# A hybrid decoder layer on one core: the order of w_in's column pairs, and where the RWKV gates, key norms and the first convolution tap are computed

## The chip, the cores and the metric
One core of a Trainium2 chip runs one launch of the kernel. The metric is the device time of that launch in microseconds, the median over several runs. In the profile TensorE is PE (its weight loads PEld), VectorE is DVE, ScalarE is ACT and GpSimd is POOL; SP issues most of the weight loads.

## The reference
One inference step of one layer, for 256 prompt tokens and 8 sample tokens (264 columns together), width 2048. Two feed-forward blocks (width 5632) enclose the token mixers:

```python
p = rms_norm(x) @ w_in            # [attn q,k,v | RWKV r,k,v,w-lora,a-lora,g-lora | conv u,B,C], 6400 columns
xm = p_rwkv + (prev - p_rwkv) * mu                     # token shift
w_log = -softplus(-(w0 + tanh(wl) @ w2)) - 0.5;  decay = exp(-exp(w_log))
a = sigmoid(a0 + al @ a2);  g = sigmoid(gl) @ g2       # the gates, 768 columns each
kk = normalised(kr * k_k);  kmod = kr * (1 + (a - 1) * k_a)
S_t = S_{t-1} diag(w_t) + (S_{t-1} a_t) b_t^T + v_t k_t^T ;  y_t = S_t r_t   # a_t = -kk, b_t = kk * a
y = groupnorm(y) * ln_w + ln_b
y_rwkv = (y + sum(r * kmod * r_k) * v) * g             # the bonus
y_conv = B * conv3(C * u)
x += concat(attention, y_rwkv, y_conv) @ w_out
```

The 256 prompt tokens of the RWKV recurrence are computed in four chunks of 64: products of keys and readers (grams), the inverse of a triangular matrix in five levels of doubling, then states and outputs. The eight samples take one step of the recurrence each.

## The kernel before
The whole layer is one stream of instructions per engine, written out by hand; semaphores order the engines. Weights come from DRAM in chunks of 512 columns of K by 256 (512 KB) into a ring of four (`raw`). ScalarE rounds each chunk to its high part (`head`, L298), VectorE makes the low part (`tail`, L304), and TensorE makes three products for each 128 x 128 tile (`products`, L317 to L319). Two 128-column tiles are a pair; w_in has 25 pairs of four chunks. A pair is 96 products.

Beside w_in's pairs the engines take other work from lists keyed by the pair (`beside` in `act_in`, `dve_in`, `pe_in`); what stands at pair i is queued behind that pair's chunks on its engine. `column_pair` gives the order of the pairs: attention (0 to 5), convolution (16 to 24), the low-rank columns (15), then receptances, keys, values (6 to 14). Each pair is scaled into `pj` by `project` (L595) and, if it is of RWKV, shifted by `dve_token_shift` (L962 to L971). The attention of the samples runs beside pairs 20 to 24: value loads are issued by ScalarE (L1144), products by `pe_sample_values` (L1084) in three triples, picked by `pe_collect_values` (L1094). The convolution's taps are VectorE's (`dve_conv_taps`: tap 2 at L933, taps 1 and 0 at L935), in pair 21.

Behind w_in comes `pe_shift`, then `pe_gates` / `act_gates` / `dve_gates`: squares and head sums of the keys (L1420), 18 gate products (L1444: six decays, six a, six g) that two banks take in turn, the spread of the head norms (L1435), kk, b, the modified keys, the bonus (L1449, L1585, L1528), scans of the decays (L1561), three Exp (L1498, L1499, L1503) and the transposes of values and readers (L1466). ScalarE also rounds attention and convolution outputs for w_out here (L1163, L899), and VectorE makes their low parts (L1273, L979). Then `pe_chunks` and its partners: grams (L1667), the levels (L1691, L1694, L1702 on TensorE, L1980 on VectorE), own values (L1709), reads (L1733), states, outputs and the group norm in two parts (sums L1867, squares L1876, spread L1885, the four VectorE steps L1915 to L1925). GpSimd does the samples' recurrence on 96 x 4096 states (L1377 to L1401) from the time the keys are ready; two of its sums are VectorE's (L2005, L2007 behind level 0, L2010 behind level 3). It writes the new states in four quarters; ScalarE's heads of w_out's first four chunks wait for one quarter each. w_out's first four chunks are loaded as soon as the ring has room.

The scratch tiles are placed by hand over each other; the ring's space is reused for the states while the ring waits.

## Time and profile before

| | us |
|---|---|
| median of 3 runs | 2160.91 (2160.15 to 2162.11) |
| the profiled execution | 2158.34 |
| its span, first to last instruction | 2156.6 |
| TensorE busy in the span | 2087.8 |
| VectorE busy | 1175.5 |
| ScalarE busy | 876.1 |
| GpSimd busy | 198.3 |

The page gives busy times, the chain that ended last and the costliest groups. The trace behind it can be asked for the chain in order of time, the instructions of one engine in a stretch, who waited for whom, and a table of stretches with the granted clock of TensorE. Since the profile was taken on one execution, its times add up to 2158.34, not to the median.

### The profile page before, as it was taken

How to read it: one execution, taken by the hardware profiler on the slowest of the kernel's cores; microseconds unless marked ns; L12 is line 12 of the kernel's file. 1: busy time of each engine (PE TensorE's matmuls, PEld its weight loads, DVE VectorE, ACT ScalarE, POOL GpSimd, SP SyncE). 2: the span in 40 equal slices, each digit the busy share in tenths (PEclk: the TensorE clock that was granted, in tenths of full speed). 3: DMA queues.
4: the chain of work that ended last, by engine and by line, in shares of the span. 5: the costliest groups of instructions: out<-in, count | busy, mean ns of one | idle time of the engine just before them, and what ended most of it. 6: DMA issues, size and time to landing. Idle time of an engine off the chain costs nothing.

```text
span 2156.6 us, 44699 instructions
## 1 busy us (share of the span) xinstructions
PE 2087.8 (97%) x18380; PEld 2048.8 (95%) x18380; DVE 1175.5 (55%) x1204; ACT 876.1 (41%) x984; POOL 198.3 (9%) x176
## 2 busy tenths in 40 slices
PE   6999999999999999999997979999999999999997
PEld 5999999999999999999984879999999999999997
DVE  5555555555444545669886455555555555544442
...
GB/s 161 181 180 183 179 183 178 182 182 179 178 184 175 178 182 192 167 214 218 282 207 39 9 105 185 177 184 180 180 183 178 183 179 181 182 174 181 195 175 90
DMA packets 359389, 373.36 MB, mean 173 GB/s; under 512 B 13397, under 2 KB 351865, under 8 KB 359206
## 3 DMA queue, kind: packets, MB, share of 16 engines
...
## 4 chain that ended last, share of the span: by engine, by line
PE 91%; DVE 5%; ACT 1%; DMA 1%; issue 1%; ACTq 0%; POOL 0%; POOLq 0%; SPq 0%; DVEq 0%
PE ps L317 29%; PE ps L319 29%; PE ps L318 28%; DVE wL L304 2%; DMA raw<-in_w_in_dram 1%; PE ps L1444 1%; DVE xL L351 0%; PE ps L1691 0%; PE ps L1694 0%; PE ps L1702 0%; PE ps L1084 0%; DMA vrowa<-in_rwkv_mu_dram 0%; PE ps L1733 0%; PE ps L1718 0%; PE ps L1435 0%
## 5 line engine op out<-in xcount | busy, mean ns | idle before, releaser
L304 DVE TENSOR_TENSOR wL<-raw,wH 128x1024 fp32r<-128x1024 f32 (+1 forms) x676 | 828.5, 1232 | 858.0 <-ACT wH L298 857.6
L298 ACT ACTIVATE wH<-raw 128x1024 fp32r<-128x1024 f32 (+1 forms) x676 | 699.9, 1038 | 1000.0 <-PE ps L319 937.3
L317 PE MATMUL ps<-xH,wH 128*128 128x264 f32 x3616 | 1030.5, 285 | 10.7 <-DVE wL L304 10.6
L319 PE MATMUL ps<-xH,wL 128*128 128x264 f32 x3616 | 1028.4, 284 | 0.0
L318 PE MATMUL ps<-xL,wH 128*128 128x264 f32 x3616 | 1028.4, 284 | 0.0
L317 PEld LDWEIGHTS ps<-xH,wH 128*128 128x128 f32 x3616 | 682.4, 189 | 14.5 <-issue 12.7
L319 PEld LDWEIGHTS ps<-xH,wL 128*128 128x128 f32 x3616 | 682.3, 189 | 0.0
L318 PEld LDWEIGHTS ps<-xL,wH 128*128 128x128 f32 x3616 | 681.6, 188 | 0.2
L317 PE MATMUL ps<-hH,wH 128*128 128x264 f32 x1408 | 402.4, 286 | 0.0
L319 PE MATMUL ps<-hH,wL 128*128 128x264 f32 x1408 | 401.5, 285 | 0.0
L318 PE MATMUL ps<-hL,wH 128*128 128x264 f32 x1408 | 401.3, 285 | 0.0
L317 PEld LDWEIGHTS ps<-hH,wH 128*128 128x128 f32 x1408 | 265.0, 188 | 0.2
L318 PEld LDWEIGHTS ps<-hL,wH 128*128 128x128 f32 x1408 | 265.0, 188 | 0.0
L319 PEld LDWEIGHTS ps<-hH,wL 128*128 128x128 f32 x1408 | 264.6, 188 | 0.0
L317 PE MATMUL ps<-mixH,wH 128*128 128x264 f32 x256 | 74.1, 289 | 5.7 <-DVE wL L304 5.7
L770 POOL DMA_DIRECT2D out_dram<-yst x8 | 5.9, 744 | 761.4 <-ACT yss L486 761.4
L318 PE MATMUL ps<-mixL,wH 128*128 128x264 f32 x256 | 73.8, 288 | 0.0
L319 PE MATMUL ps<-mixH,wL 128*128 128x264 f32 x256 | 73.8, 288 | 0.0
L392 ACT ACTIVATE st<-gt 128x528 f32<-128x528 f32 x44 | 28.5, 647 | 83.5 <-DVE gt L388 83.5
L756 POOL TENSOR_TENSOR acc<-acc,sq 128x528 f32<-128x528 f32 x21 | 31.0, 1478 | 292.6 <-ACT sq L340 292.3
L758 POOL COPY acc<-sq 128x528 f32<-128x528 f32 x3 | 2.4, 799 | 575.6 <-ACT sq L340 575.6
L317 PEld LDWEIGHTS ps<-mixH,wH 128*128 128x128 f32 x256 | 49.4, 193 | 6.2 <-DVE wL L304 6.2
...
## 6 DMA issues: line engine op xcount, KB each, us to landing
raw<-in_ffn_w_gate_dram SPq DMA_DIRECT2D x176, 512.0 KB, 3.5
raw<-in_ffn_w_up_dram SPq DMA_DIRECT2D x176, 512.0 KB, 3.5
raw<-in_ffn_w_down_dram SPq DMA_DIRECT2D x128, 512.0 KB, 3.6
raw<-in_w_in_dram SPq DMA_DIRECT2D x100, 512.0 KB, 5.0
...
raw<-in_w_out_dram SPq DMA_DIRECT2D x32, 512.0 KB, 3.9
...
```

The source lines that it names most:

```text
L298: nc.scalar.activation(wH[:, k % RING, 0:nk, :], raw[:, k % RING, 0:nk, :], ACT.Copy).then_inc(S("head_made"), 1)
L304: nc.vector.tensor_tensor(wL[:, k % RING, 0:nk, :], raw[:, k % RING, 0:nk, :], wH[:, k % RING, 0:nk, :].bitcast(F32), ALU.subtract).then_i ...
L317: nc.tensor.matmul(out, wH[:, k % RING, q, cols], high, start=a, stop=False)
L318: nc.tensor.matmul(out, wH[:, k % RING, q, cols], low, start=False, stop=False)
L319: last = nc.tensor.matmul(out, wL[:, k % RING, q, cols], high, start=False, stop=b)
L392: nc.scalar.activation(st[:], gt[:], ACT.Silu).then_inc(S("silu_made"), 1)
L756: nc.gpsimd.tensor_tensor(acc[:], acc[:], sq[:, slot, :, :], ALU.add).then_inc(S("squares_added"), 1)
L758: nc.gpsimd.tensor_copy(acc[:], sq[:, 0, :, :]).then_inc(S("squares_added"), 1)
L770: pool.dma_start(yp[:, :, bass.ds(i * (2 * CW) + jj * CW, CW)], yst[:, jj, :, :]).then_inc(S(f"y_out{jj}"), 16)
L1444: nc.tensor.matmul(ps[:, 6 + m % 2, 0:N], a, b, start=True, stop=True).then_inc(S("gates_made"), 1)
```

## The change
The 25 pairs come in another order: attention, convolution, low-rank as before, then keys, values, receptances. `seat` places keys and receptances in `pj` with their places exchanged. With that, more work is put beside pairs 19 to 24, some is put behind w_in, and some of what was in the gates goes into the levels and the group norm:

- ScalarE makes the convolution's tap 2 (the first one computed, with the bias) in pair 20, VectorE tap 1 in pair 20 and tap 0 in pair 21; `dve_conv_in` goes to pair 19, the state rows' transposes too.
- ScalarE bends the low-rank columns in pair 22, squares the keys in pair 23, and in pair 24 takes their root and evicts gates 0 to 9. TensorE sums the key squares and makes gates 0 and 1 behind pair 23's products, gates 2 to 7 between the chunks of pair 24, and 8 to 11 behind it. The decay and a gates alternate, on the two halves of the array's rows. VectorE makes the reciprocal and the scan mask in pair 24.
- The third triple of sample values and two of the three collections go behind w_in. The last r pair is shifted in two parts: the samples at once, the tokens behind the grams.
- The factor of the modified keys is ScalarE's (`kf`). The splits of attention and convolution for w_out and the samples' outputs go behind level 0, the sample sums L2005 and L2007 behind level 1, the bonus terms behind level 2; the bonus product and its shift go into the group norm.
- GpSimd's twelve issues of state rows go between the second and third of its steps on the states. It loads the spread table a second time after the g gates.
- SyncE waits with the loads of w_out for the third transition, since `kf` and `rd` lie in the ring.
- `act_rwkv_head` also waits for the second spread (`head_spread` 3).

The core of the diff (places of tiles, renamed semaphores and renamed operands left out):

```diff
-        for lo, hi, shift in ((0, 6, 0), (6, 15, 10), (15, 16, 0), (16, 25, -10)):
+        for lo, hi, shift in ((0, 6, 0), (6, 15, 10), (15, 16, 0), (16, 22, -7), (22, 25, -16)):
...
+        sp.wait_ge(S("transitions_out"), 3)
...
-            20: [lambda: act_load_values(act, (0, 1, 2))],
+            20: [lambda: act_load_values(act, (0, 1, 2)), lambda: act_conv_tap(act)],
             21: [lambda: act_sample_exp(act)],
-            23: [lambda: act_load_values(act, (3, 4, 5)), lambda: act_sample_values(act, 0)],
-            24: [lambda: act_load_values(act, (6, 7)), lambda: act_sample_values(act, 1)],
+            22: [lambda: act_bend(act)],
+            23: [lambda: act_load_values(act, (3, 4, 5)), lambda: act_sample_values(act, 0),
+                 lambda: act_key_squares(act)],
+            24: [lambda: act_load_values(act, (6, 7)), lambda: act_sample_values(act, 1),
+                 lambda: act_key_root(act), lambda: act_gate(act, range(10))],
...
-        return q if q < 6 or q == 15 else q + 10 if q < 15 else q - 10
+        return q if q < 6 or q == 15 else q + 10 if q < 15 else q - 7 if q < 22 else q - 16
+
+    def seat(q):
+
+        return 2 * column_pair(q) + (-6 if 16 <= q < 19 else 6 if q >= 22 else 0)
...
-            19: [lambda: dve_key_scores(dve, (6, 7))],
-            20: [lambda: dve_sample_max(dve), lambda: dve_conv_in(dve)],
-            21: [lambda: dve_sample_probs(dve), lambda: dve_conv_taps(dve)],
-            22: [lambda: dve_turned_sample_probs(dve), lambda: dve_conv_rows(dve), lambda: dve_conv_samples(dve)],
-            23: [lambda: dve_token_shift(dve, (15, 16, 17, 18))],
-            24: [lambda: dve_token_shift(dve, (19, 20, 21, 22, 23))],
+            19: [lambda: dve_key_scores(dve, (6, 7)), lambda: dve_conv_in(dve)],
+            20: [lambda: dve_sample_max(dve), lambda: dve_conv_rows(dve), lambda: dve_conv_taps(dve, (1,))],
+            21: [lambda: dve_sample_probs(dve), lambda: dve_conv_taps(dve, (0,)), lambda: dve_conv_samples(dve)],
+            22: [lambda: dve_turned_sample_probs(dve), lambda: dve_token_shift(dve, (15, 16, 17))],
+            23: [lambda: dve_token_shift(dve, (18, 19, 20, 21))],
+            24: [lambda: dve_token_shift(dve, (22, 23)), lambda: dve_scan_mask(dve), lambda: dve_key_scale(dve)],
...
-            19: [lambda: pe_turn_key_scores(pe)],
+            19: [lambda: pe_turn_key_scores(pe), lambda: pe_turn_state_rows(pe)],
             21: [lambda: pe_turn_sample_probs(pe)],
-            20: [lambda: pe_turn_state_rows(pe)],
             22: [lambda: pe_sample_values(pe, 0)],
-            23: [lambda: pe_collect_values(pe, 0), lambda: pe_sample_values(pe, 1)],
-            24: [lambda: pe_collect_values(pe, 1), lambda: pe_sample_values(pe, 2)],
+            23: [lambda: pe_collect_values(pe, 0), lambda: pe_sample_values(pe, 1), lambda: pe_key_sums(pe),
+                 lambda: pe_gate(pe, (0, 1))],
+            24: [lambda: pe_gate(pe, (8, 9, 10, 11))],
         }
         for i in range(3, MT // 2):
             pe.wait_ge(S("projected"), i - 1)
             for k in range(4):
                 products(pe, xH, xL, CK * k, CK, 2 * (i % 2), k == 0, k == 3, IN, IN_PER, i, k)
+                if i == 24 and k < 3:
+                    pe_gate(pe, (2 * k + 2, 2 * k + 3))
...
+    def act_conv_tap(act):
+        act.wait_ge(S("conv_state"), 2)
+        for j in range(RT):
+            nc.scalar.activation(pu[:, j, 0:T], pc[:, j, 0:T], ACT.Identity, bias=vec("cb", j), scale=vec("cw", 12 + j)
+                                 ).then_inc(S("conv_head"), 1)
...
-    def dve_conv_taps(dve):
-
-        for i in (2, 1, 0):
+    def dve_conv_taps(dve, taps):
+
+        for i in taps:
+            if i == 1:
+                dve.wait_ge(S("conv_head"), RT)
             back = 2 - i
             for j in range(RT):
                 out, src = pu[:, j, back:T], pc[:, j, 0:T - back]
-                if i == 2:
-                    ins = nc.vector.tensor_scalar(out, src, vec("cw", 12 + j), vec("cb", j), ALU.mult, ALU.add)
-                else:
-                    ins = nc.vector.scalar_tensor_tensor(out, src, vec("cw", 6 * i + j), out, ALU.mult, ALU.add)
+                ins = nc.vector.scalar_tensor_tensor(out, src, vec("cw", 6 * i + j), out, ALU.mult, ALU.add)
...
+    def dve_last_samples(dve):
+
+        q = MT // 2 - 1
+        j, s = 2 * column_pair(q) - 12, seat(q)
+        dve.wait_ge(S("projected"), q + 1)
+        dve.wait_ge(S("mixed"), 2 * (q - 15))
+        keep_shift(dve, q)
+        link(nc.vector.tensor_tensor(dif[:, :, T:N], shT[:, j:j + 2, :], pj[:, s:s + 2, T:N], ALU.subtract), dve)
+        dve.wait_ge(S("shift_columns"), q - 14)
+        mix(dve, q, dif, slice(T, N))
+
+    def dve_last_tokens(dve):
+
+        v, q = nc.vector, MT // 2 - 1
+        s = seat(q)
+        x = pj[:, s:s + 2]
+        dve.wait_ge(S("head_spread"), 1)
+        dve.wait_ge(S("decay_logs"), 6)
+        linked([
+            v.tensor_tensor(dif24[:, :, 1:T], x[:, :, 0:T - 1], x[:, :, 1:T], ALU.subtract),
+            v.tensor_scalar(dif24[:, :, 0:1], x[:, :, 0:1], -1.0, None, ALU.mult),
+        ], dve)
+        mix(dve, q, dif24, slice(0, T))
...
+        pool.wait_ge(S("gates_made"), 18)
+        pool.dma_start(hs[:], t["c_spread"]).then_inc(S("gains_in"), 16)
...
+        pool_state_rows(pool)
...
+    def pe_key_sums(pe):
+
+        pe.wait_ge(S("lora_in"), 80)
+        pe.wait_ge(S("key_terms"), 6)
         for j in range(RT):
-            last = nc.tensor.matmul(ps[0:H, 0, 0:N], hd[:, 10 - 2 * j:22 - 2 * j], t2[:, j, :],
+            last = nc.tensor.matmul(ps[0:H, 5, 128:392], hd[:, 10 - 2 * j:22 - 2 * j], ksq[:, j, :],
                                     start=j == 0, stop=j == RT - 1)
         last.then_inc(S("head_sums"), 1)
...
+    def pe_gate(pe, ms):
+
+        for m in ms:
+            j = m // 2 if m < 12 else m - 12
+            if m == 0:
+                pe.wait_ge(S("lora_in"), 80)
+                pe.wait_ge(S("lora_bent"), 2)
+                pe.wait_ge(S("sample_columns"), 2)
+            if m == 12:
+                pe.wait_ge(S("state_rows"), 3)
+            elif m == 13:
+                pe.wait_ge(S("values_out"), 5)
+            elif m >= 2:
                 pe.wait_ge(S("gates_out"), m - 1)
...
+    def pe_gates(pe):
+        pe.wait_ge(S("lora_in"), 80)
+        pe.wait_ge(S("head_scale"), 1)
+        pe.wait_ge(S("gates_out"), 12)
+        for j in range(RT):
+            if j == 4:
+                pe.wait_ge(S("projected"), MT // 2)
+            last = nc.tensor.matmul(ps[:, SPREAD[j], 0:N], hs0[:, j * P:j * P + P], hn[:], start=True, stop=True)
+        last.then_inc(S("head_spread"), 1)
+        pe_collect_values(pe, 1)
+        pe_sample_values(pe, 2)
+        pe_collect_values(pe, 2)
+        pe_shift(pe)
+        pe_gate(pe, range(12, 18))
+        pe.wait_ge(S("mixed"), 14)
+        pe.wait_ge(S("kk_made"), 4)
+        turn_tokens(pe, pvr, 0, 6)
...
+    def act_key_squares(act):
+        act.wait_ge(S("mixed"), 8)
+        for j in range(RT):
+            nc.scalar.activation(ksq[:, j, :], pkr[:, j, :], ACT.Square, scale=vec("kk", j)
+                                 ).then_inc(S("key_terms"), 1)
...
+    def act_gates(act):
+        ex = nc.scalar.activation
+        act_gate(act, (10, 11))
+        act_sample_values(act, 2)
+        act.wait_ge(S("tables_in"), 32)
+        for m in Zq:
+            identity(m)
+        act_keep_picked(act)
+        act_shift(act)
+        act_gate(act, range(12, 18))
         act.wait_ge(S("decay_logs"), 7)
-        act.wait_ge(S("kk_made"), 1)
-        ex = nc.scalar.activation
         ex(aT[:, :, 0:T], aT[:, :, 0:T], ACT.Exp, scale=-DECAY).then_inc(S("decays"), 1)
-        ex(t1[:, :, 0:T], lc[:, :, 0:T], ACT.Exp, scale=DECAY).then_inc(S("decays"), 1)
+        ex(gr[:, :, 0:T], lc[:, :, 0:T], ACT.Exp, scale=DECAY).then_inc(S("decays"), 1)
+        act.wait_ge(S("chunk_used"), OUT)
+        act.wait_ge(S("gates_out"), 12)
+        for j in range(RT):
+            ex(kf[:, j, :], aa[:, j, :], ACT.Identity, bias=omk[:, j:j + 1], scale=vec("ka", j)
+               ).then_inc(S("key_terms"), 1)
         ex(svec[:, 1, :].rearrange("p (b j) -> p j b", b=NB), sw[:, :, T:N], ACT.Exp, scale=-DECAY
...
+        ex(rd[:, :, 0:T], lc[:, :, 0:T], ACT.Exp, scale=-DECAY).then_inc(S("decays"), 1)
+        act.wait_ge(S("decays"), 3)
+        act.wait_ge(S("mixed"), 20)
         stage(1)
...
+    def dve_keys(dve):
+
+        link(nc.vector.tensor_tensor(pkr[:, :, 0:T], pkr[:, :, 0:T], kf[:, :, 0:T], ALU.mult), dve)
+
+    def dve_grown_keys(dve):
+
+        nc.vector.tensor_tensor(quarters(bk[:])[:, :, :, 0:4:3, :], quarters(pairs(pkr), 2), quarters(pairs(gr), 2),
+                                ALU.mult).then_inc(S("decayed"), 1)
+
+    def dve_reads(dve):
+
+        v = nc.vector
+        link(v.memset(zero[:], 0.0), dve)
+        dve.wait_ge(S("decays"), 3)
+        link(v.tensor_copy(wc[:], rd[:, :, C - 1:T:C]), dve)
+        dve.wait_ge(S("mixed"), 22)
+        v.tensor_tensor(rd[:, :, 0:T], pr[:, :, 0:T], rd[:, :, 0:T], ALU.mult).then_inc(S("decayed"), 1)
+
+    def dve_bonus(dve):
+
+        dve.wait_ge(S("decayed"), 4)
+        for j in range(RT):
+            ins = nc.vector.scalar_tensor_tensor(pkr[:, j, :], pr[:, j, :], vec("rk", j), pkr[:, j, :], ALU.mult, ALU.mult)
+        ins.then_inc(S("bonus_made"), 1)
...
+        pe_bonus(pe, 0)
         pe_group_squares(pe, 0)
         pe_group_sums(pe, 1)
         pe_group_spread(pe, 0)
+        pe_bonus(pe, 1)
...
 def act_rwkv_head(act, part):
         act.wait_ge(S("rwkv_made"), part + 1)
+        act.wait_ge(S("head_spread"), 3)
...
+        dve_keys(dve)
+        dve.wait_ge(S("grams_made"), 2)
         dve_gram(dve, 2, Aq[0], SL, 4)
+        dve_grown_keys(dve)
         dve.wait_ge(S("grams_made"), 3)
         dve_level(dve, 1)
+        dve_gram(dve, 4, Aq[1], SL, 6)
+        dve.wait_ge(S("decays"), 3)
         dve_gram(dve, 5, Aak[0], SU, 4)
-        dve_gram(dve, 4, Aq[1], SL, 6)
         dve_gram(dve, 6, Aak[1], SU, 6)
+        dve_last_tokens(dve)
+        dve_reads(dve)
...
             if lv == 0:
+                dve_split_attention(dve)
+                dve_sample_out(dve)
+                dve_split_conv(dve)
+            if lv == 1:
                 dve.wait_ge(S("sample_parts"), 1)
                 v.tensor_reduce(smal[:, 0:C], S2[:, :, 0:C // 2], AX.X, ALU.add).then_inc(S("sample_sums"), 1)
                 dve.wait_ge(S("sample_parts"), 2)
                 v.tensor_reduce(smal[:, C:C + 2], ycat[:], AX.X, ALU.add).then_inc(S("sample_sums"), 1)
+            if lv == 2:
+                dve_bonus(dve)
+                dve_split_samples(dve)
...
+        dve_bonus_values(dve, 0)
         dve_group_scale(dve, 0)
         dve_group_centre(dve, 1)
         dve_group_gate(dve, 0)
+        dve_bonus_values(dve, 1)
```

## Rows read from the trace of the kernel before

**Rows 1.** Page, part 1: busy us, share of the span, instructions.
```profile
PE 2087.8 (97%) x18380; PEld 2048.8 (95%) x18380; DVE 1175.5 (55%) x1204; ACT 876.1 (41%) x984; POOL 198.3 (9%) x176
```

**Rows 2.** Stages; length, PE, PEld, DVE, ACT, POOL busy, clock, DMA share, GB/s.
```profile
1140.00:1165.00 25.00, 19.13 (x50) 11.38 (x49) 17.39 (x29) 13.66 (x24) 5.98 (x10) 0.73 0.03 6
1165.00:1187.00 22.00, 14.63 (x317) 12.54 (x319) 13.42 (x11) 10.34 (x16) 10.62 (x4) 0.74 0.05 15
```

**Rows 3.** Chain that ended last, in order of time: start, us, what.
```profile
1115.61 0.32 PE ps L317
...
1127.41 0.79 PE ps L1094 x8
1128.21 2.72 PE ps L1084 x12
...
1182.44 1.59 PE ps L1667 x48
...
1187.49 1.47 PE ps L1691 x6
...
1217.95 2.83 PE ps L1733 x48
...
1272.13 0.59 PE ps L317
```

**Rows 4.** TensorE's waits from 1000 to 1131: us in total, times, longest.
```profile
PE ps L317 <- DVE wL L304: 3.5, 2, 2.5
```

**Rows 5.** Timeline of VectorE: start, us, what, times.
```profile
1077.36 2.01 DVE L933 TENSOR_SCALAR pj<-pj,vcol 128x256 f32<-128x256 f32 x6
...
1174.02 1.75 DVE L1591 TENSOR_TENSOR bk<-pj,t 128x1536 f32<-128x1536 f32 x1
...
1194.43 2.27 DVE L2005 TENSOR_REDUCE smal<-S 96x64 f32<-96x2048 f32 x1
...
1209.77 1.05 DVE L1980 COPY_PREDICATED zz<-cm,ps 128x768 f32<-128x768 uint32 x1
```

**Rows 6.** Timeline of ScalarE and its queue.
```profile
1115.66 3.73 ACTq L1144 DMA_DIRECT2D vb<-in_cache_swa_v_dram  x6
...
1138.06 1.28 ACT L1481 ACT_TABLE_LOAD   x1
1139.35 0.38 ACT L1481 ACTIVATE hn<-ps 12x264 f32<-12x264 f32 x1
...
1161.84 1.48 ACT L1498 ACTIVATE aT<-aT 128x1536 f32<-128x1536 f32 x1
...
1177.08 1.63 ACT L1514 ACTIVATE early<-ps 64x768 f32<-64x768 f32 x2
...
1180.22 2.53 ACT L1528 ACTIVATE bv<-bv,vcol 128x264 f32<-128x264 f32 x6
```

**Rows 7.** Timeline of TensorE; two instructions (passes) make one float32 product.
```profile
911.83 1.94 PE L1001 MATMUL ps<-rq,cb 128*128 128x264 f32 x8
...
1144.42 5.45 PE L1435 MATMUL ps<-hn,hs 12*128 12x264 f32 x12
1149.80 10.31 PE L1444 MATMUL ps<-pj,lora 64*128 64x264 f32 x24
```

**Rows 8.** Timeline of GpSimd.
```profile
1138.51 3.96 POOL L870 DMA_DIRECT2D out_dram<-zoT  x8
...
1177.83 8.90 POOL L1377 TENSOR_TENSOR S<-S,sv 96x4096 f32<-96x4096 f32 x1 [4.44 <-DVE pj L1594]
...
1205.87 4.55 POOL L1376 TENSOR_TENSOR S<-S 96x2048 f32<-96x2048 f32 x1
```

**Rows 9.** Timeline of TensorE, group norm.
```profile
1262.99 1.98 PE L1885 MATMUL ps<-hn,hs 12*128 12x136 f32 x12 [2.00 <-DVE hn L1908]
```

**Rows 10.** Windows of TensorE alone: length, busy, clock, DMA share, GB/s.
```profile
1006.00:1008.00 2.00, 2.00 (x11) 0.50 0.78 182
```

**Rows 11.** Page, part 6: DMA issues, KB each, median us to landing.
```profile
raw<-in_w_out_dram SPq DMA_DIRECT2D x32, 512.0 KB, 3.9
```

419 lines of the change are left out of this document (211 added, 208 removed).

## The prediction
> **What bounds the kernel now.** I read the page first: TensorE is busy 97% of the span [rows 1], so the only time to be had is where it works below its pace. The stage table shows such a place: behind w_in TensorE's mean clock is 0.73 and 0.74 of full, so about half of the time at 1.2 GHz, and of those 47 us 13 hold no TensorE work at all [rows 2]. The chain of work gives the landmarks [rows 3]: pair 24's products end at 1127.4, the loop over the five levels of the inverse starts at 1187.5 (60.1 us later), w_out's first product is at 1272.1 (84.6 us after that). The change is to the 60.1 us: work that only needs keys, gates or the low-rank columns is done beside w_in, where ScalarE and VectorE have room, and what only needs receptances or attention is put off into the level loop. I follow four stretches: (a) pairs 20 to 24, (b) the end of w_in to the level loop, (c) the levels, (d) the group norm up to w_out. Before and after each stretch I ask what arrives last.
>
> **(a) Pairs 20 to 24.** TensorE waits for VectorE's tails here in only two places, 3.5 us in all, and 2.5 of it once [rows 4]: in pair 21, behind 18 tap instructions and the sample probabilities. The first tap (6 instructions, 2.0 us [rows 5]) goes to ScalarE, whose Identity with a bias costs about 0.42 each (6 in 2.53 us [rows 6]). Tap 1 goes into pair 20, and there VectorE now waits for ScalarE's six, which are queued behind nine issues of value loads (at 3.73 us for six [rows 6], 5.6 us). So VectorE leaves pair 20 some 0.7 us late and the 2.5 us wait shrinks by 0.8, not by 2.0. Ends: 0 and 2.5. If it grew, the cover would have to be gone in pair 21 again; I see no room for more than 0.5 us of loss.
> Added to TensorE: six head sums of key squares and gates 0 to 7 before pair 24's last product, gates 8 to 11 behind it. A 264-column float32 product of two passes takes 1.94/4, overhang off 0.45 us, at full clock [rows 7]. Head sums: 6 x 0.45 = 2.7 us. Gates 0 to 7: 8 x 0.45 = 3.6 us.
> Added wait: gate 2 needs gate 0's bank back from ScalarE. In this pair ScalarE first issues six value loads, 1115.7 to 1119.4 [rows 6], copies sample values (0.6), loads the Sqrt table (1.28 [rows 6]) and takes the root (0.4), loads the Sigmoid table (1.28) and evicts (0.5): ready at 1119.4+0.6+1.7+1.8 = 1123.5. TensorE arrives there at 1115.6 + 2.7 + 0.9 (gates 0, 1) + 2.95 (a fourth of a pair: 1115.6 to 1127.4 [rows 3]) = 1122.1, with the same 0.8 taken off both. So a stall of 1.4, with semaphores 1.7 us; ends 0 and 4. Behind the waiting gate stand three quarters of pair 24, and nobody else. ScalarE's eviction of later gates (0.5 each, two per 2.95 us) is hidden.
> The Trainium skill ("ScalarE: Activation LUTs", section What ACT_TABLE_LOAD costs) gives 1.28 us for a load and as much as 1.38 us of drain before it. By the page the stall would be 2.8 us longer. The row has the load alone, with the next activation right behind it [rows 6], so the trace does not show the drain on an engine that has run dry.
> Sum of (a): -0.8 + 2.7 + 3.6 + 1.7 = +7.2: pair 24's products end at 1134.6 instead of 1127.4.
> The head sums, gates, key squares and the root leave stretch (b), where they ran at a worse clock: the spreads took 5.45 for six products and twelve gates 10.31 [rows 7], against 2.7 and 5.4 at full clock.
>
> **(b) From there to the level loop.** TensorE: gates 8 to 11, 1.8 + 0.3 for the eviction, then six spreads 2.7 (1139.4), picking sample values 0.8, the last two samples' values 2.7 (both at their duration in the chain [rows 3]): 1142.9. From here ScalarE is the engine that arrives last, and I add up its queue: copy 0.6, two identities 1.6, picked values 0.5, three state row copies 0.7, six g gates 4.4 (taken between 0.5 and 0.9 each; 0.86 is what they cost at half clock [rows 7]), Exp table 1.28, two Exp over all tokens 2.9 (1.48 each [rows 6]), six key factors 2.5, a small and a third Exp 1.6, two stages of values 3.2 (1.63 each [rows 6]), two reader copies and one of sample vectors 2.0. Small copies are put at the 0.25 to 0.8 that their size gives at the rate of the rows. Sum 21.3, with 0.7 of latencies: 1164.9 when the last values are staged. VectorE's scans, kk, bT and the readers fit beside that: they need 3.6 + 2.6 + 1.8 + 1.8 us after 1135.5 and are wanted at 1152. The first gram is at 1163.3; VectorE then has, on the path, level 0 (1.1), keys (1.75), the mask of a gram (0.95) and the grown keys (1.75 [rows 5]), with latencies 1169; then two grams of keys, 1.59 each [rows 3], with a mask between them: level loop at 1172.4. The last r pair's token part and the reads (4.2 us) stand behind it on VectorE and cost level 0 what I count in (c).
> The clock: TensorE has four lines of low-row products and waits here, and in the kernel before it ran at 1.2 GHz for half of this time. Up to 1142.9 I priced full clock. If it falls before the sample values, they and the spreads cost up to 5.4 more. I take 1.5 (nearest is the row of spreads at 5.45 behind similar gates). Level loop at 1173.9: 13.6 us earlier than 1187.5. Ends: 9 and 17.
> The rule for pairs of gates: an even gate uses rows 0 to 63 of the array and an odd one rows 64 to 127, in two banks. The Trainium skill ("TensorEngine Tiling (Array Packing)", section When to Use Tiling) has two such products run side by side. By the page ten gates would cost 2.2 us less. No row here has this pair of forms at this size, so the sum doesn't use it.
>
> **(c) The levels.** In the kernel before, the reads of chunk 0 began at 1218.0 [rows 3], 30.5 us after the level loop's start. VectorE now has between levels: the split of attention, sample outputs and the split of the convolution (1.2 + 0.6 + 1.9 against a pause of 3.2 us), and at the start the reads. That costs 0.4 + 0.7 + 0.35 = 1.4 us. The bonus products (2.6) fit into the pause behind level 2.
> GpSimd is what I expect to arrive last. Its state work starts with the grown keys, 3.3 us before the level loop (before: 9.7 us before it, 1177.83 [rows 8]). Two passes 8.9 + 4.55 [rows 8], then the twelve issues of state rows, moved into this chain: eight take 3.96 [rows 8], twelve 6.1. Then 0.5, and again 8.95 + 4.55. Third part ready at -3.3 + 13.5 + 6.1 + 0.5 + 13.6 + 0.4 of latencies = 30.8 us after the loop's start. VectorE waits for it behind level 3, with the last level's copies queued behind: reduce 2.27, copy 1.05 [rows 5], so TensorE can start the reads at +34.2, against +30.5 before: 3.7 us given back, the 1.4 within it. Ends 1.4 (GpSimd in time) and 6. What hides the rest is the product of own values, which needs no copy of level 4. The vectors' way through DRAM and back starts at 1162, with the first reader copies, and I take it to end before the grown keys are made.
> GpSimd's last state write ends 53 us behind that third part, at 1258 with its landing; ScalarE needs it only for w_out's fourth chunk, after 1262. It stays hidden by 4 us or more.
> SyncE: w_out's first four loads no longer start during pair 23 but with the third transition, 25 us before w_out. A load of 512 KB lands 3.9 us after its issue [rows 11]; four, at 1.5 to 2 us of issue each, are there after some 10 us. Hidden by 15 us; without cover each microsecond late would be one lost.
>
> **(d) Group norm.** The bonus product, its value product and its shift move here. Part 0 is hidden in waits of TensorE (1.6 us), VectorE (1.0) and ScalarE (1.6) for each other. Part 1 puts TensorE's 1.6 us ahead of the second squares, VectorE's 1.0 ahead of the reciprocal; the second spread, which took 1.98 and ended at 1265.0 [rows 9], ends 1.0 later, and ScalarE now waits for it before the first head (0.85), which had hung on VectorE's products alone. Sum +1.9; ends 1 and 3.5.
>
> **Sum.** 13.6 - 3.7 - 1.9 = 8.0 us earlier at w_out; nothing behind it changes. The profiled execution took 2158.34 (span 2156.6 and 1.7 around it), so 2150.3; the median of the runs is 2160.91, 2.6 higher, and a timed run should show 2152.9.
>
> **Rivals.**
> Rival 1, more gain: gate pairs overlap, no stall, clock stays full up to the sample values. 2.2 + 1.7 + 1.5 more, with GpSimd's chain moving along: 13.4 us, 2147.5. For it: nothing in w_in fell below full clock in pairs 21 to 24. Against: twelve gates in 10.31 us [rows 7] show no overlap. 0.10.
> Rival 2, little gain: TensorE or ScalarE in (b) slower than added up (every handover costs more, spreads and sample values at half clock, +5), GpSimd another 2 us late. Gain about 1 to 3 us, 2159. 0.15.
> Rival 3, slower: low-row gates and the stall at gate 2 put TensorE's clock at 1.2 GHz in pair 24. The trace has this: behind a pause ahead of pair 16, weight products ran at clock 0.50 [rows 10], 11 in 2 us instead of 19. Pair 24 has 96 products, at half speed 11.8 us more. It decides from 8 us of products at half clock, two thirds of the pair; then +4 us, 2165. Against: three quarters of the time between gates is dense products, and the sample values between pairs 22 and 23 lowered nothing. 0.07.
> That the change does nothing is a part of rival 2: (b) is shortened only as far as ScalarE's queue lets it.
>
> **How the numbers follow.** My forecast (gain 4.5 to 11, 2150 to 2156.5) has 0.68. The range reaches from rival 1's time to 2159, taking in the unknown costs of (b) and (c) and rival 2's nearer half; it leaves out about 0.19. About 0.2% (4.3 us) is what a measurement of this kernel can tell from no change. Faster: 0.68 + 0.10 = 0.78; within: 0.15; slower: 0.07.
>
> **What would show it.** Pair 24 with one wait of 1 to 2 us for a gate's eviction and its products' end 7 us later than before; level loop about 39 us behind that; VectorE's third reduce waiting for GpSimd for 4 to 6 us and TensorE for 2 ahead of the reads; the second group spread 1 us later. It would be wrong if TensorE's clock is half in pair 24, if ScalarE isn't the last to arrive at 1165, or if GpSimd starts its state work later than the grown keys.

## The result, and the profile after

The changed kernel takes 2185.35 us (median of 4 runs, 2184.43 to 2187.75) against 2160.95 for the kernel before (4 runs, 2160.15 to 2162.11): ratio 1.0114, 95% interval 1.0097 to 1.0132. It is slower by 24.4 us, where 8 us less was forecast and 2159.0 was the range's upper end. The profiled execution took 2184.43 us, with a span of 2182.7.

The page's first part, to be laid beside [rows 1]: TensorE has the same work, and the span grew around it.

```profile
PE 2086.6 (96%) x18392; PEld 2050.0 (94%) x18392; DVE 1198.5 (55%) x1197; ACT 883.9 (40%) x1009; POOL 199.2 (9%) x177
```

The stage table says in which stretch. Columns: window, its length, busy time and instructions of TensorE, its weight loads, VectorE, ScalarE and GpSimd, TensorE's granted clock, DMA share, GB/s. First the kernel before: from pair 24's last product to the level loop, from there to the reads of chunk 0, from there to w_out.

```profile
1127.40:1187.50 60.10, 44.26 (x420) 28.86 (x419) 39.43 (x62) 32.67 (x52) 20.66 (x20) 0.76 0.14 35
1187.50:1218.00 30.50, 28.61 (x1118) 25.30 (x1120) 16.03 (x14) 16.86 (x22) 25.63 (x6) 0.97 0.01 2
1218.00:1272.10 54.10, 41.64 (x712) 36.55 (x712) 25.42 (x35) 15.75 (x23) 39.91 (x27) 0.93 0.11 31
```

The same three stretches of the kernel after:

```profile
1138.50:1182.20 43.70, 29.07 (x380) 20.12 (x379) 24.13 (x34) 23.25 (x38) 7.96 (x7) 0.75 0.18 46
1182.20:1242.10 59.90, 32.48 (x1121) 28.43 (x1118) 52.74 (x33) 17.02 (x22) 45.75 (x27) 0.75 0.01 3
1242.10:1297.80 55.70, 43.79 (x738) 38.89 (x736) 27.25 (x37) 19.40 (x35) 32.88 (x19) 0.93 0.21 68
```

The way to the level loop became 16.4 us shorter, as intended, and the last stretch 1.6 us longer, as forecast. The levels went from 30.5 to 59.9 us, at nearly the same number of TensorE products. VectorE is busy there for 52.7 us instead of 16.0: that is the cell to stop at, since what moved there adds up to some 10 us at its former durations. TensorE's waits in the levels (us in total, times, longest) name the same engine:

```profile
PE ps L1808 <- DVE zz L2133: 25.7, 2, 17.6
```

Two waits, 8.1 and 17.6 us, for the masks with which VectorE closes a level. The timelines of VectorE and of GpSimd (start, us, what, times) show what it did ahead of those masks:

```profile
1183.16 5.46 DVE L1022 TENSOR_TENSOR dif<-pj 128x510 f32<-128x510 f32 x1
1188.54 4.41 DVE L1023 TENSOR_SCALAR dif<-pj 128x2 f32<-128x2 f32 x1
...
1197.67 1.32 DVE L1337 TENSOR_TENSOR mixL<-pj,mixH 128x1024 fp32r<-128x1024 f32 x1
...
1210.67 20.97 DVE L1709 SCALAR_TENSOR_TENSOR pj<-pj,vcol 128x264 f32<-128x264 f32 x6
```
```profile
1179.13 8.93 POOL L1444 TENSOR_TENSOR S<-S,sv 96x4096 f32<-96x4096 f32 x1 [4.20 <-DVE bk L1693]
1188.14 4.78 POOL L1443 TENSOR_TENSOR S<-S 96x2048 f32<-96x2048 f32 x1
1192.87 0.58 POOL L885 DMA_DIRECT2D out_dram<-zoT  x1
...
1207.68 8.91 POOL L1451 TENSOR_TENSOR S<-S,sv 96x4096 f32<-96x4096 f32 x1 [7.74 <-DVE smal L2168]
1216.67 4.52 POOL L1443 TENSOR_TENSOR S<-S 96x2048 f32<-96x2048 f32 x1
1221.15 8.98 POOL L1453 TENSOR_TENSOR S<-S,sv 96x4096 f32<-96x4096 f32 x1
```

A product with a constant over **two columns takes 4.41 us**, and it ends (1192.95) where GpSimd's halving ends (1192.92). The subtraction before it ends 0.6 us, its own normal duration, behind GpSimd's first product. Once GpSimd only issues DMAs (from 1192.87) the next instructions of VectorE take their normal time. The six bonus instructions take 21 us beside three large GpSimd instructions, where 2.6 was forecast.

### The profile page after: what moved, and what is told of

The parts are those of the page before. It is cut to its first block and busy times, and to the rows that moved or that the text cites. A ratio compares the mean times of both kernels' runs of the same rounds, so it can differ in the third digit from the quotient of the medians.

```text
span 2182.7 us, 44753 instructions
## 1 busy us (share of the span) xinstructions
PE 2086.6 (96%) x18392; PEld 2050.0 (94%) x18392; DVE 1198.5 (55%) x1197; ACT 883.9 (40%) x1009; POOL 199.2 (9%) x177
## 5 line engine op out<-in xcount | busy, mean ns | idle before, releaser
L324 PE MATMUL ps<-xH,wH 128*128 128x264 f32 x3616 | 1031.6, 285 | 12.8 <-DVE wL L311 12.8
```

What stands on the lines that cost most here:

```text
L324: nc.tensor.matmul(out, wH[:, k % RING, q, cols], high, start=a, stop=False)
```

## The experiments

**Theory 1**: a VectorE instruction that takes its tensors from SBUF can't run beside a GpSimd instruction and waits for its end. **Theory 2**: those instructions wait for data. **Theory 3**: GpSimd's own chain sets the end. Each experiment is an edit of the kernel after, where nothing else is said. The ratios below are against the kernel before on the same chip (there 2159.8 to 2162.5).

**Move the waits, one at a time.** The last pair's token shift and the reads go ahead of the first gram, where VectorE is idle for 4.8 us:

```diff
         dve.wait_ge(S("decayed"), 2)
+        dve_last_tokens(dve)
+        dve_reads(dve)
         dve.wait_ge(S("grams_made"), 1)
...
-        dve_last_tokens(dve)
-        dve_reads(dve)
         for lv in range(LEVELS):
```


> The kernel after with VectorE's token shift of the last pair (L1022, L1023, L982) and its scaling of the reads (L1703) moved from behind the last gram to ahead of the first, into VectorE's 4.8 us of waiting for the first gram. Theory 1, a shared way to memory: a VectorE instruction that takes its operands from SBUF cannot run beside a GpSimd tensor instruction and waits for its end. Then 5.46 and 4.41 us of L1022 and L1023 become 0.7 and 0.2, TensorE's 8.1 us wait in level 0 goes, but the splits behind level 0 now fall on GpSimd's halving and wait for its end, and level 1 waits for GpSimd's small product behind its ten DMA issues: about 5 us less, 2180 us; the bonus still takes 21 us. Theory 2, data: the two instructions wait for a value of the last pair that comes late; then they take as long in the new place, the first gram's masks move out by it, and the time is 2185 or more. Theory 3, the order of GpSimd's own work sets the end: GpSimd's chain starts no earlier, so the time stays at 2185.

2179.37 us (ratio 1.0089, 1.0072 to 1.0105): 6 less than after, where theories 2 and 3 had nothing or a loss. The two instructions take 0.69 and 0.16 us in the new place, and the first level's mask starts 4.2 us behind the level loop's start instead of 13.7. The wait turned up where theory 1 puts it: the split behind level 0 took 5.03 us instead of 1.32 and ended 1.1 us, about its own duration, behind GpSimd's halving.

The bonus, moved from behind level 2 to behind level 1:

```diff
             if lv == 1:
+                dve_bonus(dve)
                 dve.wait_ge(S("sample_parts"), 1)
...
             if lv == 2:
-                dve_bonus(dve)
                 dve_split_samples(dve)
```


> The kernel after with the bonus product (L1709, six instructions) moved from behind level 2 to behind level 1, ahead of the reduction for which GpSimd waits, so that GpSimd has nothing under way. Theory 1 (shared way to memory): the six take 2.6 us in place of 21, TensorE's 17.6 us wait in level 3 goes, level 2 starts 2 us later, and the next to be late is the second half-sum of the sample state, for which VectorE waits some 6 us behind level 3: 12 us less, 2173 us. Theory 2 (data): the six wait for something late and do so in the new place too, 2185 or more. Theory 3 (GpSimd's chain alone sets the end): it becomes 2.6 us longer, 2188.

2176.07 us (ratio 1.0073, 1.005 to 1.0096; the runs spread from 2170.4 to 2180.6): 9 less, 3 short of theory 1, and again not the 2185 or more of theories 2 and 3. The six take 2.51 us. The missing 3 us are the 32-column sample split that stayed behind level 2: it took 7.14 us, until GpSimd's product was over, and so made level 3 late.

Both moves, with the sample split moved too:

> The kernel after with both moves: the last pair's token shift and the reads ahead of the first gram (VectorE's idle 4.8 us), bonus and the 32-column sample split behind level 1 ahead of the reduction. Theory 1 (shared way): of TensorE's two waits of 8.1 and 17.6 us neither stays; what stays is about 4 us in level 1 (the splits behind level 0 wait for the end of GpSimd's halving) and 2 us in level 4 (VectorE waits behind level 3 for GpSimd's second half-sum). From the start of the levels to the reads 39 us instead of 60: w_out starts 17 to 20 us earlier, 2166 us. Rival: GpSimd's own chain, whose last sample state must be out before w_out's first tiles are split, sets the end: it ends 12 to 14 us after what theory 1 gives for TensorE, and the time is 2173.

2165.40 us (ratio 1.0024, 1.0015 to 1.0034): theory 1 said 2166. The two moves are worth some 20 of the 24.4 us. The two lines are VectorE's wait for GpSimd's second half-sum behind level 3, which 2 us of TensorE's wait follow, and the split that still falls on the halving.

```profile
1191.50 4.30 DVE L1337 TENSOR_TENSOR mixL<-pj,mixH 128x1024 fp32r<-128x1024 f32 x1
...
1218.75 2.28 DVE L2175 TENSOR_REDUCE smy<-S 96x64 f32<-96x2048 f32 x1 [6.11 <-POOL S L1443]
```

**The other way round: the wait put into the kernel before.** One added instruction of two columns:

```diff
                 v.tensor_reduce(smy[:], S2[:, :, 0:C // 2], AX.X, ALU.add).then_inc(S("sample_sums"), 1)
+                linked([v.tensor_tensor(shT[:, 0, 0:2], shT[:, 0, 0:2], shT[:, 0, 2:4], ALU.mult)], dve)
```


> The kernel before with one VectorE instruction added behind level 3 and its reduction: a product of two columns by two columns in SBUF, on scratch (normally 0.2 us). Theory 1 (shared way): at that point GpSimd runs its third 8.9 us product (1210.4 to 1219.3), so the added instruction starts at about 1213 and ends only at 1219.4; level 4's masks, due at 1214, come 5.4 us late: 2166 us. Theory 2 (the waits of the kernel after are data waits, and such an instruction costs its duration): 2161.

2166.39 us (ratio 1.0023, 1.0009 to 1.0036), so 4 to 5 us for it. The profiled execution was the slowest of the seven, 2173.34: it was 7.6 us behind the profile of before already at the level loop, where the two programs are the same, and 7.5 us more at w_out (2.7 in the levels, 4.8 behind them, where TensorE's clock was 0.50 after a wait of 2.5 us). Its rows are good for the durations, not for the price. VectorE's and GpSimd's timelines:

```profile
1218.50 2.26 DVE L2010 TENSOR_REDUCE smy<-S 96x64 f32<-96x2048 f32 x1
1220.69 6.41 DVE L2011 TENSOR_TENSOR shT<-shT 128x2 f32<-128x2 f32 x1
```
```profile
1218.16 8.92 POOL L1385 TENSOR_TENSOR S<-S,sv 96x4096 f32<-96x4096 f32 x1
```

The reduction beside the same GpSimd product takes its normal 2.26 us; the two columns end with that product. Theory 2 has nothing to say to this.

**Change the length of GpSimd's instructions**, VectorE's program untouched:

```diff
-        step(g.tensor_tensor(S2[:], S1[:], key(0), ALU.mult))
+            for k in range(4):
+                r = slice(k * 16, k * 16 + 16)
+                ins = g.tensor_tensor(out[:, r, :], S1[:, r, :], sv[:, q, :].unsqueeze(1).broadcast_to([96, 16, C]),
+                                      ALU.mult)
```


> The kernel after with GpSimd's three products over the whole sample state (8.9 us each) cut into four instructions each and its halvings (4.7 us) into two; VectorE's program is untouched. Theory 1 in its strict form (each VectorE instruction that needs the way waits for the GpSimd instruction under way, and gets in between two): L1022 and L1023 fall from 5.46 and 4.41 us to 2.5 or less each, the six bonus instructions from 21 us to at most six times 2.4, some 13: 10 to 13 us less, 2173 us. If VectorE instead waits until GpSimd's whole run of work is over, nothing changes. Theory 2 (data) and theory 3: no change, or 1 us more for the added instructions.

2183.70 us (ratio 1.0112, 1.0095 to 1.0129): 1.7 less, hardly to be told from nothing, where theory 1 said 12. In the profiles the levels are 3.7 us shorter (56.2), and their loop starts 2.1 later. The mechanism was right, the sum was not:

```profile
1185.33 1.06 DVE L1022 TENSOR_TENSOR dif<-pj 128x510 f32<-128x510 f32 x1
1186.31 2.33 DVE L1023 TENSOR_SCALAR dif<-pj 128x2 f32<-128x2 f32 x1
1188.67 5.00 DVE L982 SCALAR_TENSOR_TENSOR pj<-dif,vcol,pj 128x256 f32<-128x256 f32 x2
1193.63 0.11 DVE L1712 MEMSET zero<- 128x64 f32 x1
1193.78 2.11 DVE L1714 COPY wc<-rd 128x24 f32<-128x24 f32 x1
...
1212.85 14.43 DVE L1722 SCALAR_TENSOR_TENSOR pj<-pj,vcol 128x264 f32<-128x264 f32 x6
```
```profile
1181.15 9.78 POOL L1452 TENSOR_TENSOR S<-S,sv 96x1024 f32<-96x1024 f32 x4 [4.18 <-DVE bk L1706]
```

Every waiting instruction now takes 2.1 to 2.5 us, one GpSimd piece, and six bonus instructions take six pieces. So one instruction of VectorE gets in per gap of GpSimd. I had counted only the two instructions of the last pair that waited before; in pieces the two mixes and the 24-column copy behind them wait as well, and that stretch, from L1022 to the first mask, stays at 12.3 us (12.7 in after). The 32-column sample split behind the bonus waits too now (2.32). The fill (0.11) doesn't wait.

With eight pieces of 1.2 us instead:

> As pieces, with GpSimd's large products cut into eight instructions of 1.2 us instead of four of 2.4. Theory P (every gap between two GpSimd instructions lets one VectorE instruction in): the six bonus instructions take at most 1.7 us each, 8 to 10 us together instead of 14.4. Theory L (with short pieces GpSimd gets hold again before VectorE does): the first of them waits for the whole run of eight, and the six take 14 us or more.

One run, 2169.63 us. The six took 8.54 us, 1.4 each: theory P. Cutting finer does pay, 16 us against after by this one run (the levels take 46.1 us and TensorE waits 11.6 us there for masks, 25.7 in after), at the price of a longer GpSimd product (10.8 us instead of 8.9).

**Which instructions wait.** Beside pieces of 2.4 us, one of each kind:

```diff
+                a, b, out = dif24[:, 0, 0:P], dif24[:, 0, P:T], dif24[:, 1, 0:P]
+                linked([v.memset(out, 1.0)], dve)
...
+                linked([v.scalar_tensor_tensor(out, a, 2.0, b, ALU.mult, ALU.mult)], dve)
```


> The kernel with the last pair's token shift and the reads ahead of the first gram, bonus and sample split behind level 1, GpSimd's large steps cut into pieces of 2.4 us, and behind level 2, beside those pieces, eight added VectorE instructions of 128 columns on scratch space, one of each kind: a fill, a reduction, a reciprocal, a copy, a product with a constant, a product of two tensors, a running sum, a product of three. Each alone takes 0.1 to 0.9 us. Theory 1a: only instructions that read two tensors from SBUF wait for a piece's end (up to 2.4 us): product of two, running sum, product of three. Theory 1b: those too that run at a raised rate with one tensor source (copy, product with a constant; L1023, which took 4.41 us, is one) wait, while fill, reduction and reciprocal do not. Theory 2 (data): none waits.

```profile
1207.24 0.17 DVE L2188 MEMSET dif<- 128x128 f32 x1
1207.44 0.42 DVE L2189 TENSOR_REDUCE dif<-dif 128x2 f32<-128x256 f32 x1
1207.89 0.95 DVE L2190 RECIPROCAL dif<-dif 128x128 f32<-128x128 f32 x1
1208.88 1.25 DVE L2191 COPY dif<-dif 128x128 f32<-128x128 f32 x1
1210.16 2.27 DVE L2192 TENSOR_SCALAR dif<-dif 128x128 f32<-128x128 f32 x1
1212.47 2.33 DVE L2193 TENSOR_TENSOR dif<-dif 128x128 f32<-128x128 f32 x1
1214.84 2.50 DVE L2194 TENSOR_TENSOR_SCAN dif<-dif 128x128 f32<-128x128 f32 x1
1217.37 2.23 DVE L2195 SCALAR_TENSOR_TENSOR dif<-dif 128x128 f32<-128x128 f32 x1
```
```profile
1205.35 9.31 POOL L1452 TENSOR_TENSOR S<-S,sv 96x1024 f32<-96x1024 f32 x4 [2.39 <-DVE smal L2183]
```

Theory 1b. Fill, reduction and reciprocal run at their own pace. Copy, product with a constant, product of two, running sum and product of three each last to the end of a piece (by the group's row, 9.31/4 us each, the pieces end near 1207.7, 1210.0, 1212.3 and 1214.7). An instruction with its tensor in PSUM doesn't wait either: the masks took 1.04 us beside GpSimd throughout. The Trainium skill states this rule ("SBUF — State Buffer", section Who interferes with whom): VectorE and GpSimd share a pair of SBUF ports as an exclusive lock, taken by copies and tensor_scalar in their two-port modes and by instructions with two SBUF inputs beside a GpSimd instruction that reads SBUF, and never by tensor_reduce. The traces agree, with the numbers above. The forecast made no use of it.

**Take GpSimd's large instructions away.** The three products and two halvings cover one row of 64, and VectorE's two sums keep their size but read the loaded state. This kernel leaves out the sample tokens' output and their new state:

```diff
-        step(g.tensor_tensor(S2[:], S1[:], key(0), ALU.mult))
+        step(g.tensor_tensor(S2[:, 0:1, :], S1[:, 0:1, :], key(0)[:, 0:1, :], ALU.mult))
```


> The kernel after with GpSimd's three 8.9 us products and two 4.6 us halvings over the sample state cut to one row of 64 (the sample state's outputs are left wrong by it; VectorE's two reductions keep their size and read the loaded state). VectorE's and TensorE's programs are those of after, in the same order. If the shared way to memory is all that failed in the forecast's step on the levels, the last pair's shift takes 0.7 and 0.2 us, the bonus 2.6, and the way from the levels' start to the reads is the forecast's 34.2 us within 2: 25 us less than after, 2160 us. If something else holds VectorE or TensorE there (data, the clock after the first wait, GpSimd's writes of the state rows), 40 us or more stay, 2166 or more.

2158.08 us (ratio 0.9975, 0.9961 to 0.9989). Its row of the stage table, level loop to reads, and two of VectorE's:

```profile
1185.50:1216.60 31.10, 29.17 (x1122) 25.81 (x1118) 25.61 (x33) 17.00 (x22) 10.82 (x21) 0.95 0.02 6
```
```profile
1187.09 0.16 DVE L1023 TENSOR_SCALAR dif<-pj 128x2 f32<-128x2 f32 x1
...
1204.01 2.49 DVE L1710 SCALAR_TENSOR_TENSOR pj<-pj,vcol 128x264 f32<-128x264 f32 x6
```

31.1 us instead of 59.9, with VectorE's program in the order of after: what is left of it costs next to nothing (30.5 before the change). GpSimd's chain went with its products, so this run alone can't tell theory 1 from theory 3; the two moves and the added instruction do. The clock in the levels (0.75 in after) is back at 0.95 too: TensorE had fallen to 0.50 behind each of its two waits (windows from 1197 to 1199 and 1233 to 1235), so the clock was a consequence.

**The stretch ahead of pair 22.** Here the forecast had TensorE's wait for VectorE shrink by 0.8 us; it grew from 1.0 to 3.4. (The texts below count the gap from the start of the product before it: 2.0 and 4.4.) TensorE's wait in the kernel after, VectorE's wait for ScalarE's taps and for the split of a weight chunk, and ScalarE's for that chunk:

```profile
PE ps L324 <- DVE wL L311: 3.4, 1, 3.4
```
```profile
1066.32 2.46 DVE L953 SCALAR_TENSOR_TENSOR pj<-pj,vcol 128x255 f32<-128x255 f32 x6 [2.02 <-ACT pj L915]
...
1076.27 1.23 DVE L311 TENSOR_TENSOR wL<-raw,wH 128x1024 fp32r<-128x1024 f32 x1 [3.96 <-ACT wH L305]
...
1085.82 4.62 DVE L311 TENSOR_TENSOR wL<-raw,wH 128x1024 fp32r<-128x1024 f32 x4
```
```profile
1075.18 1.06 ACT L305 ACTIVATE wH<-raw 128x1024 fp32r<-128x1024 f32 x1 [4.41 <-DMA raw<-in_w_in_dram]
```

Windows of TensorE alone (length, busy, clock, DMA share, GB/s) show what came with it, half clock at the start of pair 22, where 3 us hold 27 products at full clock:

```profile
1087.00:1090.00 3.00, 2.82 (x13) 0.50 0.56 154
1090.00:1093.00 3.00, 3.00 (x18) 0.62 1.06 358
```

Three experiments, each on the kernel after. The convolution's edits undone:

```diff
-            20: [lambda: act_load_values(act, (0, 1, 2)), lambda: act_conv_tap(act)],
+            20: [lambda: act_load_values(act, (0, 1, 2))],
...
-            19: [lambda: dve_key_scores(dve, (6, 7)), lambda: dve_conv_in(dve)],
+            19: [lambda: dve_key_scores(dve, (6, 7))],
```


> The kernel after with the convolution's edits alone undone: its inputs made in pair 20 again, ScalarE's tap given back to VectorE in pair 21. Theory A: these edits made the gap ahead of pair 22's products grow from 2.0 to 4.4 us (VectorE waited 2.0 us for ScalarE's taps and reached the tail late), so the gap returns to about 2.0 and the time falls by 2 us, to 2183. Theory B (what the forecast said): the tap on ScalarE frees 2.5 us of VectorE there, so undoing it costs 1 to 2 us, and the growth of the gap came from the moved loads of the sample values, which stay: 2187.

2188.32 us (ratio 1.0135, 1.0118 to 1.0152), 3 more, with a wait of 4.4: theory B on the tap. It is worth some 3 us on ScalarE, though the intervals of the two kernels overlap.

ScalarE's taps ahead of its nine value loads:

```diff
-            20: [lambda: act_load_values(act, (0, 1, 2)), lambda: act_conv_tap(act)],
+            20: [lambda: act_conv_tap(act), lambda: act_load_values(act, (0, 1, 2))],
```


> The kernel after with ScalarE's six taps of pair 20 ahead of its nine issues of value loads instead of behind them. VectorE's wait of 2.0 us for the taps goes, and the loads start 3 us later. Theory A (the gap of 4.4 us ahead of pair 22 comes from the order on ScalarE: taps late, and the value loads on the way when weight chunk (21, 3) travels, 14.0 us from issue to landing): the gap falls to 1 to 2.5 us, 2 to 3 us less than after, 2183. Theory B (the lateness of the chunk has another cause): the chunk lands as late as before and the gap stays at 4 us; 2185.

2186.57 us (ratio 1.0102, 1.0087 to 1.0116). VectorE's 2.0 us wait for the taps goes, but the chunks take up to 14.4 us to land, as before (14.0), and TensorE waits 3.8: theory B. In this trace the nine issues run between and beside the taps (issues from 1060.2 to 1065.6, taps from 1060.9 to 1063.9) and start only 0.2 us later against the weight head before them, so the new order moved the loads little.

The sample columns and the gate of the convolution back behind pair 22's first steps:

```diff
-            21: [lambda: dve_sample_probs(dve), lambda: dve_conv_taps(dve, (0,)), lambda: dve_conv_samples(dve)],
+            21: [lambda: dve_sample_probs(dve), lambda: dve_conv_taps(dve, (0,))],
...
+            22: [lambda: dve_turned_sample_probs(dve), lambda: dve_conv_samples(dve),
```


> The kernel after with one edit: the convolution's sample columns and gate (3.1 us of VectorE) behind pair 22's first steps again, as in the kernel before, instead of ahead of its tails. If these 3.1 us, not the taps, are why pair 22's products wait (4.4 us against 2.0), the gap returns to 1.5 to 2 us and the time falls by 2 us, to 2183. If the late weight chunk of pair 21 (14 us from issue to landing) is the cause, the gap shrinks by under 1 us and the time stays within 1 us.

2186.67 us (ratio 1.0126, 1.0102 to 1.015): nothing gained. In its profile TensorE's wait ahead of pair 22 is gone and the clock stays at 1.00 through pairs 22 and 23. In its place TensorE waits 2.5 us at the end of pair 23 for sample values, and its clock falls there (0.71 from 1114 to 1117):

```profile
PE ps L1136 <- DMA vb<-in_cache_swa_v_dram: 2.5, 1, 2.5
```

So the 3.1 us of convolution ahead of the tails made the wait, and the value loads are next in line behind it. The late chunk isn't needed for it: with the convolution's edits undone no chunk took more than 10.3 us, and the wait was 4.4. Why the chunk lands late in after isn't settled.

**Towards a better version.** On both_early2, GpSimd's twelve issues of state rows (the text below says ten) moved into its idle time, and the second half-sum's reduction behind level 4:

> As both_early2, with GpSimd's ten writes of the state rows moved into its idle time before the vectors are staged (6.3 us out of its chain), and the second half-sum's reduction behind level 4 instead of level 3. Theory 1: the 2 us in level 4 go, the writes were hidden behind VectorE anyway: 2 us less than both_early2, 2164. Rival (GpSimd's chain sets the end): 4 to 6 us less than both_early2.

2161.11 us (ratio 1.0002, 0.9992 to 1.0012), 4.3 less than both_early2. That is nearer to the rival than to theory 1, but the reads start in time with TensorE's fifth level here, and GpSimd's last state write leaves at 1269.8, 6 us ahead of w_out's first tail. By the two profiles the levels are 2.3 us shorter (38.1 and 35.8 us), and the way from the reads to w_out 1.6 us (57.4 and 55.8): behind its wait of 2.3 us both_early2 has TensorE's clock at 0.57 and 0.58 in the windows from 1224 to 1228, where all_early2 has 1.00. That is 3.9 of the 4.3, so the wait with the clock behind it explains it without GpSimd's chain; that chain's share, if any, wasn't separated.

On top of all_early2, the small gains product (L1419) moved away from VectorE's decays:

> all_early2 with GpSimd's small product for the norm's gains (L1419, 1.8 us) moved from the moment at which VectorE multiplies the decays (L1678, 3.0 us beside it, 1.75 alone) to between GpSimd's two vector transfers, where it waits 1.9 us for a transfer. Theory 1: L1678 returns to 1.75 us. ScalarE's chain of exponentials and stagings is later than L1678 there, so the time falls by 0.5 us at most: 2161. Rival: L1678 is what sets the grams' start, and 1.3 us go: 2160.

2161.78 us (ratio 1.0001, 0.9992 to 1.0011). L1678 fell from 3.03 to 1.76 us and nothing else moved; ScalarE's chain hid it.

On all_early2 again, the two large splits behind level 4, with GpSimd made to wait for them:

> all_early2 with the two large splits (L1337, L1031, 3.1 us) and the sample split moved from behind level 0 to behind level 4, and GpSimd waiting for them before its third large product; the small sample sums (0.9 us) behind level 1. Theory 1: TensorE's 3.4 us wait in level 1 goes, the reads start 2 to 3 us earlier than in all_early2 (1218 instead of 1221), and GpSimd's chain becomes 3 to 5 us longer. If TensorE's chain sets w_out's start: 2159. Rival: GpSimd's chain, whose last sample state must have left before w_out's fourth head, is then the later one: 2162 or more.

2161.13 us (ratio 0.9996, 0.9986 to 1.0005). The split takes 1.84 us instead of 4.13 and GpSimd waits 3.0 us for it. Neither theory's time can be told from the other's.

All together, without and with the taps first:

> All that gained so far together, as a candidate against both kernels: last pair's shift and reads ahead of the first gram, bonus behind level 1, the two large splits behind level 4 with GpSimd waiting for them, second half-sum's reduction behind level 4, state rows early, the small product for the norm's gains between GpSimd's vector transfers. The parts were worth, against all_early2 (2161.1): the splits and the small product nothing that could be told alone. Theory 1 with GpSimd's chain as the next bound: 2160, not to be told from before. If the two only hid each other: 2158.

> best2 with ScalarE's taps ahead of the value loads (as tap_first). Theory A of tap_first: 2 to 3 us less than best2, 2157 to 2158, and so faster than the kernel before by 0.1 to 0.2%. Theory B: as best2, 2160.

2161.31 us (ratio 0.9993, 0.9982 to 1.0003) and 2161.42 us (ratio 0.9989, 0.9981 to 0.9998). The last is 24 us faster than the changed kernel; against the kernel before it is 0.1% by the interval, less than what I said a measurement can tell.

**The same wait in w_in, in both kernels.** The trace of before had it all the time, in four weight tails that take 12.3 us instead of 4.6:

```profile
1027.66 12.29 DVE L304 TENSOR_TENSOR wL<-raw,wH 128x1024 fp32r<-128x1024 f32 x4
```
```profile
1028.02 3.51 POOL L1309 TENSOR_TENSOR kb<-kb,qb 128x1536 f32<-128x1536 f32 x1
...
1034.23 3.49 POOL L1309 TENSOR_TENSOR kb<-kb,qb 128x1536 f32<-128x1536 f32 x1
```

hs_later with GpSimd's key products cut in three:

```diff
-            nc.gpsimd.tensor_tensor(kb[b % 3][:], kb[b % 3][:], q, ALU.mult).then_inc(S("key_products"), 1)
+            for k in range(3):
+                ins = nc.gpsimd.tensor_tensor(kb[b % 3][:, k, :], kb[b % 3][:, k, :], qb[:, b % 2, :], ALU.mult)
```


> hs_later with GpSimd's eight key products of w_in's pairs 11 to 19 (3.5 us each) cut into three instructions each. Both kernels show VectorE's weight tails slowed beside them (four tails in 12.3 us at 1027, alone 4.6). Theory 1: each tail waits for at most 1.2 us instead of 3.5, the four take about 7 us, and TensorE's wait of 2.5 to 3.4 us for them goes: 2 to 3 us less than hs_later, 2158. Rival: the ring of four weight buffers hides the tails' lateness; within 1 us of hs_later.

2160.24 us (ratio 0.9993, 0.9983 to 1.0002), not to be told from hs_later, and four tails took 12.8 us, as uncut (12.2). And cut in two, on the kernel after:

> The kernel after with each of GpSimd's key products of w_in cut into one of 2.3 us and one of 1.2 us. Theory P, or L with 2.3 us as long enough: the first weight tail at 1027 (4.9 us beside the uncut product, 1.2 alone) gets in behind the first piece and takes 3.7 us or less. Theory K (the kind of VectorE instruction decides; tails read and write more than the bonus does): it waits for both pieces and takes 4.9 us or more, as uncut.

One run, 2185.05 us. The first tail again waited for both pieces:

```profile
1026.62 5.08 DVE L311 TENSOR_TENSOR wL<-raw,wH 128x1024 fp32r<-128x1024 f32 x1
```
```profile
1026.96 2.40 POOL L1375 TENSOR_TENSOR kb<-kb,qb 128x1024 f32<-128x1024 f32 x1
1029.31 1.29 POOL L1377 TENSOR_TENSOR kb<-kb,qb 128x512 f32<-128x512 f32 x1
```

The outcome is theory K's, but its reason doesn't hold: in probes the split L1337, of the same kind and size as a tail, took 2.44 us beside two halving pieces and got in between them. What sets these tails apart is that their record starts 0.3 to 0.5 us ahead of GpSimd's, and all the same they end behind it. Whether that start decides wasn't tried.

## Why the prediction was wrong

At w_out's first product the forecast was 8.0 us early and the kernel 25.7 us late. The 33.7 us between are 3.9 from (a), 4.4 from (b), 25.7 from (c) and -0.3 from (d).

- **(c) The levels: the step that failed.** It gave back 3.7 us by the forecast and 29.4 in fact. "The bonus products (2.6) fit into the pause behind level 2" and "the reads (4.2 us)" took VectorE's durations as properties of the instructions. They were read where GpSimd was idle or only issued DMAs; the change puts them beside [rows 8]'s products of 8.9 and 4.55 us. The working priced the new load on each engine alone and asked which arrives last; that two engines can be in each other's way didn't enter it. GpSimd as the last to arrive was wrong as well: it was VectorE for which both TensorE (25.7 us) and GpSimd (7.7 and 5.8 us) waited. Its sum of 30.8 us for GpSimd's third part has no wait for VectorE's first sum, either: with both moves made that was 3.2 us, and the part was ready 34.7 us after the loop's start (both_early2). With the large steps away, and GpSimd's chain with them, the stretch took 31.1 us, less than the 34.2 forecast.
- **(a) Pairs 20 to 24: +11.1 instead of +7.2.** The terms for TensorE's new work held or were generous: head sums 2.83 us (2.7), gates 0 to 7 four times 0.65 net (3.6 in all forecast), one wait of 1.2 for gate 0's bank (1.7). The two table loads of that wait took 1.28 us each, right behind the activation before them, so nothing of the longer stall of 2.8 us more showed. The term for pair 22 was wrong in sign: -0.8 forecast, +2.4 measured, and 2.3 more by the half clock behind the wait. Part of it was a misreading. Of the waits in [rows 4] I put the one of 2.5 us into pair 21; it lies at 1004, ahead of pair 16, and the wait ahead of pair 22 was 1.0 us, so there was never more than 1.0 to gain. The other part is the 3.1 us of sample columns and gate that the change moves ahead of pair 22's tails: I didn't price them at all. The +11.1 is that of one execution: in the profiles of kernels with the same program up to here, pair 24's last product began between 1137.9 and 1141.9 (1138.3 in after).
- **(b) To the level loop: 43.7 us instead of 39.3.** The spreads took 3.70 us (2.7), picking 1.87 (0.8) and the last values 4.42 (2.7), at a clock of 0.50 from 1144 on, 3.8 us more in all. I had put 1.5 us on the clock, with 5.4 as the far end; with the waits between them the last values ended 12.9 us behind pair 24 instead of 8.3, 4.6 later. ScalarE was the last to arrive, as forecast, and the way from the first gram to the level loop was 10.2 us (9.1). The loop started 5.3 us earlier than before; the range given for it was 9 to 17.
- **(d) Group norm: right.** +1.6 us (1.9), the second spread 0.7 us later behind the reads (1.0), w_out's loads hidden.
- **Rivals.** Rival 3 had a mechanism that is there, half clock behind a wait. In the profiled execution it struck pair 22, and pair 24 ran at 1.00 throughout. But in the profiles of both_early2, all_early2 and short_steps, whose w_in is that of after, pair 24 too had some 3.4 us at 0.50 soon behind the gate's wait of 1.3 to 1.4 us (mean clock 0.83 from 1128 to 1138 in both_early2). That is less than half of the 8 us from which the rival would have decided. Rival 1's overlap of gate pairs is there in part: four passes in 0.72 us, 0.65 net, where I counted 0.9. None of the cases held two engines in each other's way, and so the range ended 26 us too early.

Two pieces of the chain that ended last (start, us, what): ScalarE's last table load, from which on its queue holds no gap to the last staging at 1169.7, and the first gram.

```profile
1159.39 1.28 ACT L1593
...
1171.97 1.53 PE ps L1783 x48
```
